# Which queue issues the first weight piece, the vector table, x and the constants of a decoder step

## The reference, cut to what matters

```
h = rmsnorm(x, norm_mix)
xr, q, k, v, g_rnn, g_attn = split(h @ w_in)           # 1024 -> 4352 columns
y_rnn  = rg_lru(causal_conv(xr), gates from w_rg, w_ig, decay from softplus(-lru_lambda))
y_attn = window_attend(q, k, v, sinks, ALiBi)          # 16 heads, 2 of keys and values
x = x + [sigmoid(g_rnn) * y_rnn, sigmoid(g_attn) * y_attn] @ w_out
x = x + moe(rmsnorm(x, norm_ffn))                      # 32 experts, top 4, clamped SwiGLU
y = rmsnorm(x, norm_final)
```

## Time and profile before

| | |
|---|---|
| runs | 1146.99, 1147.6 and 1148.8 us, median 1147.6 |
| profiled execution | 1147.16 us |
| its span, first to last instruction | 1145.4 us |
| around the span | 1.76 us |
| mean granted clock of TensorE | 0.998 |
| TensorE busy | 1113.8 us, 97% |
| read from HBM | 436.00 MB, 383 GB/s over the span with the writes |

### The profile page before, as it was taken

The page is one execution under the profiler, slowest core; times in us unless marked ns, Lnnn a source line. Parts: engine busy times, 40 slices in busy tenths (PEclk is TensorE's granted clock), DMA queues, the critical chain, the costliest instruction groups (busy, mean ns, idle before and its releaser), DMA issues.

```text
span 1145.4 us, 14895 instructions
## 1 busy us (share of the span) xinstructions
PE 1113.8 (97%) x5772; PEld 493.7 (43%) x5772; DVE 311.7 (27%) x785; ACT 229.3 (20%) x642; POOL 33.8 (3%) x69
## 2 busy tenths in 40 slices
PE   9999999999999999999999999999999999999997
PEld 6687778844343424333333333333232323232432
DVE  6665543032131221212130303121212030312123
ACT  4564363422020202010101111111111101010103
POOL 0200012210000000000000000000000000000000
PEclk9999999999999999999999999999999999999999
DMA  9743636999999999999999999999999999999996
GB/s 349 281 142 107 187 112 270 391 375 427 428 427 427 426 427 427 427 429 427 429 428 429 429 428 429 429 428 428 429 429 429 428 428 429 429 428 425 427 426 244
DMA packets 39650, 437.90 MB, mean 382 GB/s; under 512 B 6592, under 2 KB 8912, under 8 KB 10944
## 3 DMA queue, kind: packets, MB, share of 16 engines
q1 hardware_dynamic: 38984, 435.65, 91.3%
q10 hardware_dynamic: 624, 1.68, 0.4%
HBM read 436.00 MB, written 2.41 MB: 383 GB/s over the span
## 4 chain that ended last, share of the span: by engine, by line
PE 69%; DMA 24%; DVE 3%; ACT 2%; issue 1%; DVEq 0%; SPq 0%; ACTq 0%
PE bank L1284 21%; DMA ring<-in_w_down 20%; PE bank L1328 19%; PE bank L1041 8%; PE bank L1086 5%; PE bank L1184 4%; DMA area<-in_w_down 3%; PE bank L1205 3%; PE bank L1134 2%; PE bank L1218 1%; PE bank L1181 1%; PE bank L1022 1%; PE bank L1208 1%; DVE area L1719 1%; PE bank L909 1%
## 5 line engine op out<-in xcount | busy, mean ns | idle before, releaser
L1284 PE MATMUL bank<-ring,area 128*64 128x512 f32 x1824 | 414.0, 597 | 9.8 <-DMA ring<-in_w_up 9.6
L1284 PEld LDWEIGHTS bank<-ring,area 128*64 128x64 f32 x1824 | 122.6, 136 | 273.3 <-issue 234.4
L1328 PE MATMUL bank<-ring,area 128*64 128x512 f32 x848 | 194.2, 598 | 6.4 <-DMA ring<-in_w_down 6.4
L1707 DVE TENSOR_TENSOR x_tok<-x_tok,bank 128x512 f32<-128x512 f32 x60 | 41.3, 688 | 328.0 <-PE bank L1205 328.0
L786 ACT ACTIVATE area<-area 128x256 f32<-128x256 f32 x64 | 26.7, 417 | 514.2 <-DVE area L1719 514.2
L1041 PE MATMUL bank<-ring 128*128 128x264 f32 (+1 forms) x512 | 121.7, 393 | 0.0
L1328 PEld LDWEIGHTS bank<-ring,area 128*64 128x64 f32 x848 | 57.8, 136 | 110.3 <-issue 92.4
L1041 PEld LDWEIGHTS bank<-ring 128*128 128x128 f32 x512 | 95.2, 190 | 21.3 <-issue 4.0
L1744 DVE TENSOR_TENSOR area<-area 128x1024 f32<-128x1024 f32 x15 | 18.4, 1225 | 211.3 <-ACT area L796 211.3
L1205 PE MATMUL bank<-area 128*128 128x512 f32 x128 | 71.8, 644 | 0.0
L1086 PE MATMUL bank<-area,ring 128*128 128x264 f32 x256 | 58.6, 387 | 0.0
(11 more groups left out here) (271 smaller groups left out, 712.6 us busy)
## 6 DMA issues: line engine op xcount, KB each, us to landing
ring<-in_w_up SPq DMA_DIRECT2D x112, 2048.0 KB, 33.2
ring<-in_w_down SPq DMA_DIRECT2D x49, 2048.0 KB, 31.6
area<-in_w_up SPq DMA_DIRECT2D x12, 2048.0 KB, 27.2
area<-in_w_down SPq DMA_DIRECT2D x11, 2048.0 KB, 31.8
ring<-in_w_in SPq DMA_DIRECT2D x16, 1024.0 KB, 9.4
ring<-in_w_out SPq DMA_DIRECT2D x8, 1024.0 KB, 4.9
ring<-in_w_down SPq DMA_DIRECT2D x7, 1024.0 KB, 37.1
area<-in_w_up SPq DMA_DIRECT2D x4, 1024.0 KB, 7.0
```

The lines of the kernel that those rows point to most:

```text
L1284: m = mm(bank[2 * h + n][64 * e:64 * e + 64, :], xe[:, k, 64 * e:64 * e + 64], w[:, kk, e, NB * n:NB * (n + 1)], start=False, stop=(k == K ...
L1328: m = mm(bank[4 + c][64 * e:64 * e + 64, :], y_t[:, 4 * half + f, 64 * e:64 * e + 64], w[:, f, e, :], start=False, stop=(half == 1 and f = ...
L1707: eng.tensor_tensor(x, x, combined_bank(unit, last)[:, :], ALU.add).then_inc(s.added, 1)
```

## The change

SP no longer issues the vector table and the first weight piece. It begins with the first piece of x, then the second piece of x, then the second weight piece, and then goes on as before. ACT issues the first weight piece and the vector table, in this order, ahead of everything else it does. The issue of the constants moves from behind the dummy exponential to behind the exponential of lambda. The warm-up has 12 matmuls instead of 14.

```
@@ block.sync
-            eng.dma_start(vec[:, :], vec_cols).then_inc(s.rows_loaded, 16)
             head = blocks[:, trunk_slot(0), :]
             for part, sem in enumerate((s.head_loaded0, s.head_loaded1)):
                 c, k = slice(2 * COLS * part, 2 * COLS * (part + 1)), slice(2 * part, 2 * part + 2)
-                eng.dma_start(head[:, c], w_in[0][:, c]).then_inc(sem, 16)
                 eng.dma_start(x_raw[:, k, :], x_cols[:, k, :]).then_inc(sem, 16)
+                if part:
+                    eng.dma_start(head[:, c], w_in[0][:, c]).then_inc(sem, 16)
             eng.dma_start(x_raw[:, KB // 2:, :], x_cols[:, KB // 2:, :]).then_inc(s.xr_loaded, 16)
@@ block.scalar
+            eng.dma_start(blocks[:, trunk_slot(0), 0:2 * COLS], w_in[0][:, 0:2 * COLS]).then_inc(s.head_loaded0, 16)
+            eng.dma_start(vec[:, :], vec_cols).then_inc(s.rows_loaded, 16)
             eng.wait_ge(s.consts_set, 2)
             act(stat[:, 15:16], eps[:, :], ACT.Exp)
-            eng.dma_start(keep[:, :], c_in[:, 0:C_KEEP]).then_inc(s.consts_loaded, 16)
...
             eng.wait_ge(s.sp_step, 3)
             act(sm[:, 8:16], sm[:, 0:8], ACT.Exp).then_inc(s.sp_exp, 1)
+            eng.dma_start(keep[:, :], c_in[:, 0:C_KEEP]).then_inc(s.consts_loaded, 16)
             eng.wait_ge(s.head_loaded1, 32)
@@ block.tensor
             eng.wait_ge(s.zeroed, 1)
-            keep_warm(14, bank[7])
+            keep_warm(12, bank[7])
```

## The result

The changed kernel takes 1157.34 us (median of four, 1156.61 to 1159.16), the kernel before 1147.76 us in the same comparison: ratio 1.0082, 95% interval 1.0069 to 1.0094. It is 9.6 us slower, where I had forecast 1147.3 us and no change that can be measured. Its profiled execution took 1159.16 us, with a span of 1157.3 us. That span is 11.9 us longer than the one of before, and the following looks for these 11.9 us; the execution profiled is the longest of the four, and so they are more than the 9.6.

A forecast was written before the change was run, and what follows sets the result against it. TensorE has 69% of the chain, DMA 24%; in the expert stage TensorE waits for weights. Of 1.0 us gained at the start 0.7 becomes a wait: 1147.16 - 0.3 = 1146.86, with 0.44 for the median 1147.3 us; range 1145.7 to 1148.8.

The forecast's parts named there:

- Step 4: Warm-up at the start: two matmuls fewer cost nothing; warm-up ends at 5.5 us, TensorE idles 0.9 us, clock stays high.
- rival (e): Something unseen moves the expert stage by over 2 us, in either direction; chance 0.06.
- slower by over 0.2%: Whole kernel: chance 0.03 of a measurable slowdown, 0.2% being 2.3 us; within that 0.94.
- no part of it has a time of its own: Expert stage: weights' transfers wait for slots TensorE empties, so an earlier trunk end moves the whole stage with it.
- Step 1: Start: x issued first, with 224 KB fewer bytes up to it, lands at 5.6 us instead of 6.59.
- Step 2: Start: vector table behind ACT's weight piece lands at 5.6 us; TensorE starts 1.0 us earlier, at 6.3 to 6.4.
- rival (d): Start: table lands at 6.5 us or later, TensorE starts no earlier; 1147.5 to 1147.7 us, chance 0.08.
- Step 3: ACT's start: two transfers issued first delay the dummy exponential by up to 0.8 us; covered by idle time, cost nothing.
- Steps 5 and 6: Start: second x piece at about 7.6 us, covered by 0.1 us; constants at 10, bounds 9.0 to 15.7, no wait.
- Rival (c): Before k = 7: constants land after 14.2 us, costing 1.5 us at 15.7, less 0.3 gained; 1148.8 us, chance 0.06.
- What was late next: Before k = 4: rest of first weights gains 0.3 us on 11.1; 0.7 of the 1.0 us becomes a wait.
- rival (b): Start: the whole gain of 1.0 us, up to 1.3, is carried to the end; 1146.3 to 1146.6 us, chance 0.15.

The follow-up runs named there:

- e2: The changed kernel with 14 warm-up matmuls again, so only the transfers are moved against the kernel before; 1148.17 us, ratio 0.9998.
- e1: The kernel before with 12 warm-up matmuls instead of 14 and nothing else; 1158.8 us, ratio 1.0088.
- e4: The kernel before with four instead of six warm matmuls ahead of the experts, its start kept; 1158.05 us, ratio 1.0084.
- e3: The changed kernel with two matmuls added where the trunk ends, ahead of the last token rows; 1148.47 us, ratio 1.0006.
- e5: The kernel before with 13 warm-up matmuls; 1157.67 us, ratio 1.0082.
- e7: The changed kernel with 14 warm-up matmuls and the vector table first on SP, ACT keeping the first weight piece alone; 1147.06 us, ratio 0.9990.
- e11: The kernel before with the constants issued behind the exponential of lambda and nothing else; 1147.44 us, ratio 0.9999.
- e9: The kernel before with 54 warm-up matmuls, the loop 80 instructions further on; 1160.11 us, one execution.
- e10: The kernel before with 110 warm-up matmuls, the loop 192 instructions further on; 1173.0 us, one execution.
- e6: The kernel before with 16 warm-up matmuls; 1147.97 us, ratio 0.9997.

## Why the prediction was wrong

**What failed.** Step 4, "two warm-up matmuls fewer ... cost nothing". Its price was 9.6 us (with the two matmuls back in place, e2, nothing is left of it), and not for the warm-up's sake. I costed the two matmuls as time at the start and never asked what else in the kernel depends on their being there as instructions. e1 and e4 show that two matmuls taken out ahead of the loop cost this in either of two places over 200 us apart, e3 that two put in at a third place heal it. The rival (e), "something I don't see", had a chance of 0.06, and with it "slower by over 0.2%" had 0.03.

**Could it have been seen?** In part. The list of queues shows q8 with 28 packets over the run, and none from 520 to 1000 us in the kernel before; a loop that runs that long without fetches is held whole, and what is held whole may just fit. 284 matmuls and as many weight loads in a pair make 1704 instructions in a turn, by the counts of the profile's groups, with waits and register work still to add. That the top lay at a boundary no row of before shows; e5 was needed. The chance for a second-order effect of the code's length should have been given with a mechanism and a place.

**The expert stage.** Whether no part of it has a time of its own, as I wrote, the runs leave open for small shifts (e7: 0.99 us at block 1, 1.07 at pair 5, 0.77 at pair 15, 1.1 with a wide interval by the ratio). And I read it as bound by weights throughout. The pairs' starts show two regimes, 54.97 us by TensorE up to 728 us and 58.7 by the weights behind that. That is why 32 us of stalls and slow matmuls cost only 12: the rest was paid for with waits for weights that fell away.

**Step 1, x first.** The mechanism was right and the term mis-sized: in the changed kernel the first x piece, issued at 0.75, landed 3.9 us later, at 4.65, for 5.6 forecast, and the first weight piece at 5.75. Neither helped, as the table came later. In e7, where the table is issued ahead of x, x landed at 5.48 and was what TensorE waited for.

**Step 2, the table.** The term was mis-sized. I took 4.4 us from issue to landing, inside a range of 2.2 to 4.9; it took 5.57. It landed at 6.77, beyond the 6.5 that rival (d) asked for, and TensorE began at 7.47, no earlier than before. Rival (d), at 0.08, is what the start did, and its 1147.5 to 1147.7 is what e2 shows: 1148.17 us, even with the kernel before at 1148.28. The row I relied on was for pieces of 256 KB on SP's queue; the table came behind one on the second queue.

**Step 3, ACT's own work,** cost nothing, as said: the dummy exponential ran at 2.98 and the first scaling at 6.80.

**Step 4, the clock.** Wrong in the changed kernel. The warm-up ended at 5.08, TensorE idled 2.38 us instead of the forecast 0.9, as the table was late, and the matmuls began at the low level: 8.35 us for 6.89. These are the 1.5 us of the start in the profiled execution.

**Steps 5 and 6.** The second pieces were ready at 7.97 for 7.6 forecast, and k = 2 was not held up by them. The constants landed at 7.42 + 6.4 = 13.8, not at 10, between my bounds, 2 us ahead of their use only because the start was late; in e7 they held TensorE for 0.28 us. Rival (c)'s mechanism is real; its price there was smaller than the 1.5 us I gave.

**What was late next.** The rest of the first weights landed at 2.62 + 8.0 = 10.6 in the changed kernel, 10.8 forecast. In e7, with the table out of the way, it came at 10.0 and 0.99 of the 1.12 us gained at the start reached block 1, as in rival (b); in e11 only the constants were moved and the gain went into waits, as in the forecast. The Trainium skill, DMA: Bandwidth & Descriptors, section "Issuing engines are not separate DMA queues", would leave nothing to the second queue but issue time. The traces agree as far as they can tell: from 2 to 7 us the eight profiles with SP's order of before have 237 to 276 GB/s, 257 in the mean, and the six with the first weight piece on ACT 267 to 288, 280 in the mean. The difference is 0.12 MB, which 0.45 us move at 257 GB/s, and one issue takes SP 0.47 us.

## What to carry to other kernels

An instruction taken out or put in ahead of a long loop can cost far more than its own time: here its place alone decided whether each turn brought the loop's code in anew, which fits a loop that barely fits into what the engine holds. Compare the packets of the instruction queues before and after every change, look for waits for "issue" at the loop's first instructions, and when they appear, move the loop by a few instructions before looking for another cause. And when a small transfer that everybody needs was put behind a large one in its queue, it landed after it (44 KB behind 256 KB: 5.6 us, ahead of it 3.3): of the data at a start, try the smallest and most used first.

## What the runs showed of the hardware that I had not expected

**Return to code that is not there.** Each return waited about 3 us for code in e9 and e10 (3.13 and 2.77 at the first), where the next boundary is far from the top, and 7.8 to 8.7 us in the four kernels with 12 or 13 warm-up matmuls or with 4 ahead of the experts, where it is next to it, while the data queues were loaded at 427 GB/s. Whether it would be less beside idle data queues no run shows.

**The clock of a start.** The point where the warm-up matmuls go from 0.43 to 0.21 us apart differed from kernel to kernel with the same first microsecond: after the one begun at 3.54 in the changed kernel, at 3.96 in e1 and e6, at 4.39 before, and in e3 all 12 went at the low level, up to 5.9 us, and in e2 all 14, up to 6.9. e3's matmuls nevertheless began at the high level 1.72 us later. e1's warm-up was over at 5.24, it idled 2.04 us and began at the low one. Granted clocks of e1 at 7.4 to 8.4 us and of e3 at 7.6 to 8.6 us:

```profile
7.40:8.40 1.00, 1.00 (x3) 0.75 (x4) 0.00 (x0) 0.00 (x0) 0.00 (x0) 0.51 0.98 383
```

```profile
7.60:8.60 1.00, 0.99 (x4) 0.85 (x5) 0.60 (x2) 0.82 (x3) 0.00 (x0) 1.00 0.97 388
```

Behind idle times of up to 1.72 us the first projection began at the high level in all kernels profiled, behind 2.04 and 2.38 us at the low one in both. The length of the idle time alone doesn't decide: at the returns of e9 the clock was 1.00 behind a wait of 3.06 us (688 to 690 us) and 0.54 behind one of 2.95 us (857 to 859 us). So in the profiled executions two matmuls fewer in the warm-up cost 1.5 us at the start in two kernels and nothing in a third. That the third kernel's own executions lie in two groups 2 us apart suggests that this changes from one execution to the next.
